# A pooling branch moved onto TensorE, with its neighbour means as products with a banded constant, and later reciprocals in axial attention

## The reference, cut to what matters

```python
ya = global_axial_attention(qa, ka, va, gq, gk)  # 8 query heads, 2 key/value heads, qk norm, rotary
yb = pool_mixer(u, w_pool, pool_scale)

# pool_mixer, for group g of 128 channels with window w = 2, 4, 8, 16
lo = clip(t - w // 2, 0, S); hi = clip(t + w - w // 2, 0, S)
mean = (cs[:, hi] - cs[:, lo]) / (hi - lo)        # cs: cumulative sum of u over tokens
diff = mean - u
out_g = (diff @ w_pool[g]) * pool_scale_g
```

## Time and profile before

| what | value |
|---|---|
| median of 3 runs | 3155.56 us (3153.17 to 3160.29) |
| profiled execution, its own time | 3161.49 us |
| its span | 3159.6 us |
| TensorE, VectorE, ScalarE, GpSimd busy | 96%, 44%, 25%, 53% |
| pool stage, first u matmul to first axial score, layer 0 and 1 | 1320.16 to 1371.27, 2246.41 to 2296.70 us |
| mean granted clock of TensorE | 0.983 of 2.4 GHz |

### The profile page before, as it was taken

The page is one execution under the profiler, slowest core; times in us unless marked ns, Lnnn a source line. Parts: engine busy times, 40 slices in busy tenths (PEclk is TensorE's granted clock), DMA queues, the critical chain, the costliest instruction groups (busy, mean ns, idle before and its releaser), DMA issues.

```text
span 3159.6 us, 44388 instructions
## 1 busy us (share of the span) xinstructions
PE 3033.1 (96%) x14692; PEld 2387.0 (76%) x14692; DVE 1399.9 (44%) x2391; ACT 792.1 (25%) x1451; POOL 1660.6 (53%) x1254
## 2 busy tenths in 40 slices
PE   8998999999899999989999999999889999999998
PEld 6767888886578888756678878888657688878886
DVE  3254444223444442452533476640744334576622
ACT  3342221113332210144421122210253411132201
POOL 4334666663156667423346656666323266646674
PEclk9998999999999999999999999999999999999999
DMA  6262223322022233211312222333112222223232
GB/s 161 77 173 67 93 94 106 110 90 74 21 73 93 97 102 110 70 34 53 102 61 99 83 75 95 99 104 103 48 41 75 67 90 100 83 73 100 94 115 77
DMA packets 99603, 274.90 MB, mean 87 GB/s; under 512 B 38126, under 2 KB 38894, under 8 KB 99490
## 3 DMA queue, kind: packets, MB, share of 16 engines
q1 hardware_dynamic: 97328, 269.07, 26.6%
q10 hardware_dynamic: 2162, 4.36, 0.8%
HBM read 269.66 MB, written 11.54 MB: 89 GB/s over the span
## 4 chain that ended last, share of the span: by engine, by line
PE 70%; DVE 3%; ACT 2%; issue 2%; DVEq 0%; ACTq 0%
PE PA L470 11%; PE PA L472 10%; PE PA L471 10%; PE PB L470 9%; PE PB L472 8%; PE PB L471 8%; PE O L736 2%; PE S L693 2%; PE T L604 2%; PE O L502 1%; DVE tmps L1398 0%; DVE hl L1359 0%; PE PB L753 0%; ACT probs L1128 0%; DVE strip L1782 0%
## 5 line engine op out<-in xcount | busy, mean ns | idle before, releaser
L452 POOL TENSOR_TENSOR wl<-raw,wh 128x1024 fp32r<-128x1024 f32 (+2 forms) x416 | 1128.0, 2711 | 33.4
L449 POOL TENSOR_TENSOR zero<-zero 128x1 f32<-128x1 f32 x416 | 82.7, 199 | 1434.3 <-PE PA L472 703.2
L470 PE MATMUL PA<-hh,wh 128*128 128x512 f32 x1392 | 567.1, 407 | 26.4 <-DVE hl L1359 7.1
L472 PE MATMUL PA<-hh,wl 128*128 128x512 f32 x1392 | 550.0, 395 | 0.0
L471 PE MATMUL PA<-hl,wh 128*128 128x512 f32 x1392 | 550.0, 395 | 0.0
L450 POOL CAST wh<-raw 128x1024 fp32r<-128x1024 f32 (+2 forms) x416 | 476.3, 1145 | 0.0
L470 PEld LDWEIGHTS PA<-hh,wh 128*128 128x128 f32 x1392 | 266.5, 191 | 135.5 <-issue 67.4
L470 PE MATMUL PB<-hh,wh 128*128 128x512 f32 x896 | 357.8, 399 | 0.0
L472 PE MATMUL PB<-hh,wl 128*128 128x512 f32 x896 | 349.4, 390 | 0.0
L471 PE MATMUL PB<-hl,wh 128*128 128x512 f32 x896 | 349.2, 390 | 0.0
L472 PEld LDWEIGHTS PA<-hh,wl 128*128 128x128 f32 x1392 | 265.8, 191 | 57.5
(11 more groups left out here) (314 smaller groups left out, 4750.2 us busy)
## 6 DMA issues: line engine op xcount, KB each, us to landing
raw<-in_w_up SPq DMA_DIRECT2D x176, 512.0 KB, 3.5
raw<-in_w_down SPq DMA_DIRECT2D x64, 768.0 KB, 4.1
raw<-in_w_merge SPq DMA_DIRECT2D x48, 768.0 KB, 4.1
raw<-in_w_out SPq DMA_DIRECT2D x32, 512.0 KB, 3.5
strips_na<-in_rpb SPq DMA_DIRECT2D x1, 7620.0 KB, 32.2
raw<-in_w_pool SPq DMA_DIRECT2D x12, 512.0 KB, 3.4
raw<-in_w_na_qk SPq DMA_DIRECT2D x12, 512.0 KB, 3.5
raw<-in_w_na_v SPq DMA_DIRECT2D x8, 512.0 KB, 3.6
```

The costliest lines, as they stand in the source:

```text
L449: nc.gpsimd.tensor_tensor(zero[:, :], zero[:, :], zero[:, :], ALU.add)
L452: nc.gpsimd.tensor_tensor(wl[s][:, 0:width], raw[s][:, 0:width], wh[s][:, 0:width].bitcast(F), ALU.subtract).then_inc(w_split, 1)
L470: mm(dst, h_, rh, start=first, stop=False)
L472: return mm(dst, l_, rh, start=False, stop=last)
```

## The change

It keeps the function and changes how the pooling branch is computed and where some steps stand.

- u is projected with **tokens on partitions**: `hh`/`hl` tiles are the stationary operand, 512 weight columns are moving, and the four token tiles go to S0, S1, T0, T1 (`pool_tokens`; the weights are laid out as for the other value projections). The values of `axial_kv` move to PA instead.
- ScalarE copies the four tiles to `V`, times the token factor.
- **Mean minus u** is, for each group, seven full-precision matmuls of `V` (stationary, 128x128) with a banded constant (moving, 136, 144, 16, 112, 16, 16 and 136 columns), into the banks that the projection left (`pool_band`). All shifted adds, edge corrections and subtractions of VectorE go. It keeps one subtraction for each group that forms the remainder.
- The constant, 128 x 4 x 3 x 144 float32 (885 KB), is loaded in each layer by a transfer that ScalarE issues, since it lies under buffers used elsewhere. The small edge table goes.
- The mixers write O0, O1, T0, T1. The query's sum stands between the second and third band group, and its rotation between mixer 0 and mixer 1. The key's sum stands behind the second and its rotation behind the fourth entry of u.
- **Axial attention**: the first group's reciprocals are spread in slot 15 instead of 11 and the second's in slot 23 instead of 19, as the diff writes them below; the query's square moves from slot 4 to 3; `q_turn` waits for one copy fewer.

```diff
-Y_TURN["axial"] = (11, 19, 27, 35)
+Y_TURN["axial"] = (15, 23, 27, 35)
-TURN = dict(scale=3, square=4, sum=5, cosine=5, turn=6, root=6, invert=7)
+TURN = dict(scale=3, square=3, sum=5, cosine=5, turn=6, root=6, invert=7)
 # den_turn
-                    pe.wait_ge(pb_taken, b["b"] + 2 + min(g + 1, 3) + 1)
+                    pe.wait_ge(pb_taken, b["b"] + 2 + min(g + 2, 3) + 1)
 # q_turn
-                pe.wait_ge(den_copied, b["dc"] + b["turn"] - 1)
+                if b["turn"] > 2:
+                    pe.wait_ge(den_copied, b["dc"] + b["turn"] - 2)
+            def pool_tokens(b, kv):
+                pe.wait_ge(s_taken, b["u"] + 2)
+                pe.wait_ge(pt_copied, b["u"] + 2)
+                for e in range(4):
+                    s = e % 2
+                    pe.wait_ge(w_split, b["e"] + e + 3)
+                    for k in (2 * e, 2 * e + 1):
+                        W = wh[s][:, k % 2 * S:k % 2 * S + S], wl[s][:, k % 2 * S:k % 2 * S + S]
+                        for t, bank in enumerate(POOL_U):
+                            c = slice(t * P, t * P + P)
+                            mm(bank[:, :], hh[:, k, c], W[0], start=(k == 0), stop=False)
+                            mm(bank[:, :], hh[:, k, c], W[1], start=False, stop=False)
+                            last = mm(bank[:, :], hl[:, k, c], W[0], start=False, stop=(k == DT - 1))
+                            if k == DT - 1 and t < QT - 1:
+                                last.then_inc(pool_u, 1)
+                    last.then_inc(entry_done, 1)
+                    if e == 0:
+                        tokens(kv)
+                    if e == 1:
+                        k_sum(kv["b"] + 1, kv["r"])
+                turn_rotate(kv["b"] + 1, kv["r"], tmp[2][:, :])
+            def pool_band(b, g):
+                if g == 0:
+                    pe.wait_ge(band_in, 16 * (b["l"] + 1))
+                    pe.wait_ge(u_copied, b["pl"] + QT)
+                for n, (t, lo, hi) in enumerate(BAND_PARTS):
+                    at = lo - (t * P - REACH)
+                    last = mm(POOL_U[g][:, lo:hi], V[:, t, g * P:g * P + P], band[:, g, (t > 0) + (t == QT - 1), at:at + hi - lo],
+                              start=(n == 0), stop=(n == len(BAND_PARTS) - 1))
+                last.then_inc(band_ready, 1)
-                pool_u(0); k_sum(kv["b"] + 1, kv["r"]); tokens(kv)
-                pool_u(1); turn_rotate(kv["b"] + 1, kv["r"], tmp[2][:, :])
-                pool_u(2); pool_u(3)
+                pool_tokens(b, kv)
+                pe.wait_ge(v_copied, 4 * kv["v"] + 4)
                 project(PA[:, :], 0, b["e"] + 4).then_inc(entry_done, 1)
-                for g, bank in enumerate((S0, S1, T0, T1)):
-                    pe.wait_ge(pool_split, b["pl"] + g + 1)
-                    last = three(bank[:, :], wsl(1, g), (yh[:, 4 + g, :], yl[:, 4 + g, :]), True, True)
-                q_sum(ax["b"], ax["r"]); turn_rotate(ax["b"], ax["r"], turned_q)
+                pool_band(b, 0); pool_band(b, 1)
+                q_sum(ax["b"], ax["r"])
+                pool_band(b, 2); pool_band(b, 3)
+                pool_mix(b, 0)
+                turn_rotate(ax["b"], ax["r"], turned_q)
+                pool_mix(b, 1); pool_mix(b, 2); pool_mix(b, 3)
 # ScalarE
+                act.wait_ge(entry_done, bk["e"] + 2)
+                act.dma_start(band[:, :, :, :], consts["band"]).then_inc(band_in, 16)
+                for t, bank in enumerate(POOL_U):
+                    A(V[:, t, :], bank[:, :], ACT.Copy, scale=rsT[:, t:t + 1]).then_inc(u_copied, 1)
 # VectorE
-                front(0)
+                def remainder_of(g):
+                    dve.wait_ge(pool_hi, b["pl"] + g + 1)
+                    TT(yl[:, 4 + g, :], POOL_U[g][:, :], yh[:, 4 + g, :].bitcast(F), ALU.subtract).then_inc(pool_split, 1)
                 axial_values(kv)
                 k_norm(cols[:, bass.ds(CAT["gain_k"] + l * CPER, 1)], kv["b"] + 1, kv["r"])
-                remainders(0)
-                front(1)
                 turn(1.0, kv["b"] + 1, kv["r"], axial_key[:, :])
-                remainders(1)
-                for g in (2, 3):
-                    front(g); remainders(g)
                 scale_q({"q_at": b["e"] + 5 + 2})
                 q_cosine(ax["r"])
+                remainder_of(0); remainder_of(1)
+                link(v.reciprocal(rq_of[0], rq_root))
+                remainder_of(2); remainder_of(3)
+                turn(-0.125, ax["b"], ax["r"], q_sb[:, :])
```

More of the change, by code:

```diff
@@ L226, in build @@
         region.close()
+        region = ExitStack()
+        sb("under_band", [P, DT, S], F, region)
+        band = sb("band", [P, 4, 3, BAND], F, region)
+        region.close()
         fence = sb("fence", [P, 2 * FT * S])
@@ L318, in build @@
         block = ctx.enter_context(nc.Block())
-        NTABLE, NFIRST = 8, 5
+        NTABLE, NFIRST = 7, 5
         def difference_bank(g):
@@ L955, in axial_kv @@
                     W = wsl(s, k % 4, 2 * P)
-                    for t, bank in enumerate((S0, S1, T0, T1)):
+                    for t in range(QT):
                         c = slice(t * P, t * P + P)
-                        mm(bank[:, 0:P], hh[:, k, c], W[0], start=(k == 0), stop=False)
-                        mm(bank[:, 0:P], hh[:, k, c], W[1], start=False, stop=False)
-                        mm(bank[:, 0:P], hl[:, k, c], W[0], start=False, stop=(k == DT - 1))
+                        mm(PA[:, c], hh[:, k, c], W[0], start=(k == 0 and t == 0), stop=False)
+                        mm(PA[:, c], hh[:, k, c], W[1], start=False, stop=False)
+                        mm(PA[:, c], hl[:, k, c], W[0], start=False, stop=(k == DT - 1 and t == QT - 1))
                     last = three(PB[:, :], wsl(s, k % 4, 2 * P, P), hs(k), k == 0, k == DT - 1)
@@ new lines, in pool_mix @@
+            def pool_mix(b, g):
+                if g == 0:
+                    pe.wait_ge(w_split, b["e"] + 5 + 3)
+                pe.wait_ge(pool_split, b["pl"] + g + 1)
+                last = three(POOL_Y[g][:, :], wsl(1, g), (yh[:, 4 + g, :], yl[:, 4 + g, :]), True, True)
+                last.then_inc(*((pool_out, 1) if g < 3 else (entry_done, 1)))
+            def pool_tiles(b, kv, ax):
+                pool_tokens(b, kv)
+                pe.wait_ge(v_copied, 4 * kv["v"] + 4)
+                project(PA[:, :], 0, b["e"] + 4).then_inc(entry_done, 1)
+                pool_band(b, 0); pool_band(b, 1)
[4 more added lines that the diff above has]
+                pool_mix(b, 1); pool_mix(b, 2); pool_mix(b, 3)
@@ L1294, in _ @@
             with act.Fori(0, LAYERS2) as l:
-                bk = H("axial_kv", l)
+                bk, b, ax = H("axial_kv", l), H("pool", l), H("axial", l)
+                act.wait_ge(entry_done, bk["e"] + 2)
+                act.dma_start(band[:, :, :, :], consts["band"]).then_inc(band_in, 16)
                 sum_root(bk)
                 turn_square(pb_taken, bk["b"] + 2); k_root(bk["r"])
[L1299 to L1302, removed]
-                gain = cols[:, bass.ds(CAT["gain_q"] + l * CPER, 1)]
-                q_square(b["a"] + 6, gain)
-                for g, bank in enumerate((S0, S1, T0, T1)):
+                act.wait_ge(v_copied, 4 * bk["v"] + 1)
+                for t, bank in enumerate(POOL_U):
+                    if t < QT - 1:
+                        act.wait_ge(pool_u, 3 * l + t + 1)
+                    else:
+                        act.wait_ge(entry_done, b["e"] + 6)
+                    A(V[:, t, :], bank[:, :], ACT.Copy, scale=rsT[:, t:t + 1]).then_inc(u_copied, 1)
+                gain = cols[:, bass.ds(CAT["gain_q"] + l * CPER, 1)]
+                q_square(b["a"] + 2, gain)
+                for g, bank in enumerate(POOL_U):
+                    if g == 2:
+                        q_root(ax["r"])
+                    act.wait_ge(band_ready, b["pl"] + g + 1)
+                    A(yh[:, 4 + g, :], bank[:, :], ACT.Copy).then_inc(pool_hi, 1)
+                for g, bank in enumerate(POOL_Y):
                     if g < 3:
@@ L1937, in shape_constants @@
     aa = pos * fa[d % 16][:, None]
-    edge = np.zeros((P, 4, 16), f)
+    band = np.zeros((P, 4, 3, BAND), f)
     for g, w in enumerate((2, 4, 8, 16)):
         c = (np.clip(t + w - w // 2, 0, S) - np.clip(t - w // 2, 0, S)).astype(f)
-        edge[:, g, :8], edge[:, g, 8:] = w / c[:8], w / c[-8:]
+        for kind, tile_at in enumerate((0, 1, QT - 1)):
+            i = (tile_at * P + np.arange(P))[:, None]
+            to = (tile_at * P - REACH + np.arange(BAND))[None]
+            inside = (to >= 0) & (to < S)
+            window = inside & (i >= to - w // 2) & (i < to + w - w // 2)
+            band[:, g, kind] = window / c[np.clip(to, 0, S - 1)] - (inside & (i == to))
     return {
@@ L2011, in weight_streams @@
         mixers = np.pad(a["w_pool_2"][l].transpose(1, 0, 2).reshape(1, P, 512), ((0, 0), (0, 0), (0, 512)))
-        per["pool"].append(np.concatenate([stationary(pu), qs[:1], mixers]))
```

(1 more changed line is left out.)

59 lines of the change are left out of this document (16 added, 43 removed).

## The result

The changed kernel takes 3119.32 us, median of 4 runs (3117.95 to 3122.49), against 3155.33 before (3153.17 to 3160.29). The ratio is 0.9893, with a 95% interval of 0.9881 to 0.9904. The forecast was 3128 with a range of 3112 to 3144: the direction is right, and the gain is 36.0 us where 27.8 was forecast.

The account below looks back on a forecast made before the run. TensorE, busy for 96% of the span, was taken to bound the kernel. Gains of 12.0 + 5.1 + 7.8 + 2.9 = 27.8 us off 3161.5 gave 3133.7; less 5.9 for the median, 3128 us, range 3112 to 3144.

Parts of the forecast that it names:

- What bounds the stage: Pool stage: VectorE is the fuller engine, 41.5 of 51.2 us against TensorE's 40.4, and TensorE waits for it.
- The stage's sum: Pool stage after the change, TensorE's own terms: 44.7 us against 51.1 and 50.3, gaining 12.0 us in two layers.
- term for the switches: Pool stage: changing between two operand kinds, six switches one way and five the other, 2.9 us a layer.
- 44 to 46 us: Sign of being right: length of the pool stage after the change, with a clock of 1.00.
- The bands: Pool stage: 28 new full-precision products a layer at 0.245 us each, 6.9 us; bounds 4.3 and 15.4.
- Does anything wait: Pool stage after the change: key, copies, bands, query and mixers hold TensorE up nowhere; nothing taken for waits.
- Behind the stage: First scores after the pool stage run at full clock: 2.6 and about 2.5 us, 5.1 us gained.
- Attention, the waits: Axial attention: old turn waits go, new 2.4 us waits for the root in slots 15 and 23; 7.8 us gained.
- Attention, the clock: Axial attention: clock falls behind the 2.4 us waits cost 5.9 us; half counted as gain, 2.9 us.
- a clock of 0.5 in slots 16 and 24: Axial attention: sign of being wrong, half clock in the slots behind those of the spread.
- The square: Axial attention: the query's square one slot earlier removes a 1.2 us wait of the first turn, 2.4 in two layers.
- The table load: ScalarE in attention: 1.28 us before the root, by the row; the skill's 2.66 would take 5.5 us of gain, 3134.

Follow-up runs that it names:

- filled kernel: Kernel before with extra products that nobody reads, put where TensorE stands in the pool stage: 3149.0 us, ratio 0.9982.
- The two band experiments: Changed kernel with each band group's seven products issued twice: 3132.5 us; changed kernel without the three 16-column parts of each group: 3112.0 us.
- one slot more: Changed kernel with the axial reciprocals spread in slots 16, 24, 28 and 35 and a wait ordering each spread behind the copy before: 3108.5 us.
- the kernel with doubled bands: Changed kernel with each band group's seven products issued twice into the same bank, the second time from a fresh start: 3132.5 us.
- wide parts only: Changed kernel without the three 16-column parts of each band group: 3112.0 us.

## Why the prediction was right, and where it was off

- **What bounds the stage.** Right: it was VectorE and the waits for it. At nearly full clock the filled kernel's stage is as long as before, and with VectorE's work halved it is 9.7 and 8.9 us shorter. With the bands, TensorE sets its length, and never stands.
- **The stage's sum.** Its term for the switches was mis-sized. It took 2.9 us a layer. Measured are 41.4; less 29.9 (projections and mixers), 6.4 (bands) and 4.7 (first start 0.4, key's sum 0.87, token factor 0.90, two rotations of 0.86, query's sum 0.82) that leaves 0.4. The 0.35 read as the price of a switch into full precision held a wait for the square, 0.19, that stands in the very row. The slow matmul behind a full-precision one was counted twice, as the way back and in that product's own price: 0.46 to the next start and 0.64 to the one behind it are together the 0.87. So the stage came below the 44 to 46 us that were to show the forecast right, and gave 18.6 us in two layers, not 12.0. This is nearly all of the miss.
- **The bands.** 0.245 forecast, 0.226 to 0.236 measured. The sum of columns was taken as 576 a group and is 560, which changes only the lower bound. The Trainium skill (TensorE: Matmul & The Clock Gate, The mechanism) has loads overlap only in other row groups, and names a background weight buffer beside it. The two band experiments disagree with the first: 14 parts with 28 loads of 0.19 took 3.17 us.
- **Does anything wait.** Right: nothing did. That the rotation ahead of mixers 1 to 3 hides the last VectorE passes is shown by the rotation put last.
- **Behind the stage.** 5.1 forecast, 2.9 and 2.7 measured. Right, and by the clock, as the fill shows.
- **Attention, the waits.** Turn waits gone, a new wait of 2.3 (forecast 2.4) in slots 15 and 23: right. They were to give 7.8; TensorE stands for 6.3 us less.
- **Attention, the clock.** 2.9 forecast, 3.4 measured, as TensorE's busy time in attention (9.0 less) without the 5.6 behind the stage. The size is right, the reason is partly luck. The prediction named a clock of 0.5 in slots 16 and 24 as a sign of being wrong, and it is there behind three of the four new waits, as often as before. Half was counted without a row for it; the falls came as often and cost less.
- **The square.** It was priced at 1.2 in one turn. With the other waits gone it would have cost all three turns and their clock, 21.8 us. The change moved it, so the sum was not hurt.
- **The table load.** 1.28 us, and the root is issued at once. The 2.66 of the Trainium skill (ScalarE: Activation LUTs, What ACT_TABLE_LOAD costs) would have put the new waits at 3.7 (an estimate); the rows have 2.3.
- **Offset.** The profiled execution before was 5.9 over its median, and this was rightly taken off.

## What to carry to other kernels

Where one stage's fullest engine is not the kernel's, moving its work to the kernel's fullest engine can pay: 28 short products (6.4 us) bought 9.7 and 8.9 us. Price a short stand by the clock behind it too, and look at whether another engine would take the gain back. After moving a step, read what it waits for in its new slot: one slot more was worth another 11 us.

## What the runs showed of the hardware

TensorE can be wholly busy and still fall to half clock. In layer 1 of the kernel with doubled bands nothing waits, and yet (timeline, then windows):

```profile
2256.70 6.53 PE L1012 MATMUL S<-band,V 128*128 128x136 f32 x56
...
2263.88 11.20 PE L1012 MATMUL T<-band,V 128*128 128x136 f32 x56
```

```profile
2240.00:2260.00 20.00, 20.00 (x102) 16.71 (x101) 9.45 (x7) 4.29 (x7) 11.59 (x10) 1.00 0.16 53
2263.80:2281.00 17.20, 17.20 (x74) 14.99 (x76) 4.95 (x9) 3.77 (x8) 0.24 (x2) 0.60 0.00 1
```

The second pair of groups, the same 56 records, takes 11.2 us instead of 6.5. The window is busy throughout, at a mean clock of 0.60. What the engine did before it fell was 6.5 us of short full-precision products; layer 0 did the same and kept 2.4 GHz. This was the slowest of the kernel's four executions, 6.1 us above their median. What sets the two layers apart is open.

The same chance shows at a short wait. In eleven of the twelve profiled executions TensorE stands for 1.2 us ahead of layer 1's key and value projection, and what it did in the 7 us before is the same to 0.02 us. In nine of them the clock stays at 1.00, and from the projection's start to the first u matmul 22.9 us pass. In two, attention's edits alone and wide parts only, it falls to 0.50 some 2 us behind the stand, and 26.1 us pass. The twelfth, with the square in slot 4, stands for 2.2 us there and also takes 26.1. So a pair of traces can differ by 3 us where the code is the same.
